# Two layers of a streaming encoder: a product, two squares and the last transposes issued in another order, and the output stored in eight half rows

## The reference

```python
for i in range(DEPTH):                    # DEPTH = 2
    if i % 2 == 0:
        x = x + s5_mixer(rmsnorm(x, s5_norm[j]), ...)       # state-space layer
    else:
        x = x + retention_mixer(rmsnorm(x, ret_norm[j]), ...)
    x = x + swiglu(rmsnorm(x, ffn_norm[i]), w_gate[i], w_up[i], w_down[i])
return rmsnorm(x, final_norm)

def swiglu(u, w_gate, w_up, w_down):      # hidden width 2816 = 22 tiles of 128
    h = silu(u @ w_gate) * (u @ w_up)
    return h @ w_down
```

## Times and profile before

| | us |
|---|---|
| median of 3 runs | 1261.93 |
| lowest, highest | 1260.85, 1262.49 |
| the profiled execution, device time | 1260.84 |
| its span | 1259.1 |
| PE busy, share of the span | 1219.4, 97% |
| VectorE busy | 856.3, 68% |
| ScalarE busy | 532.7, 42% |
| GpSimd busy | 64.1, 5% |

### The profile page before, as it was taken

How to read it: one execution, slowest core, us unless ns; L and a number is a source line. 1 busy time by engine, 2 the same in 40 slices (tenths; PEclk the granted TensorE clock), 3 DMA queues, 4 the chain that set the end, 5 groups by cost and what they waited for, 6 DMA issues and landing times.

```text
span 1259.1 us, 18813 instructions
## 1 busy us (share of the span) xinstructions
PE 1219.4 (97%) x7693; PEld 1071.1 (85%) x7693; DVE 856.3 (68%) x1009; ACT 532.7 (42%) x693; POOL 64.1 (5%) x84
## 2 busy tenths in 40 slices
PE   3889999999999999999999999999999999999997
PEld 3778879889988998888888888888879899989986
DVE  8997778578857867746555565643577578857865
ACT  5655555335523544333343333422454235523532
POOL 5950000000000000000000000000000000000000
PEclk9999999999999999999999999999999999999998
DMA  5663332323332323313323133233323333333321
GB/s 117 156 124 102 100 101 76 125 67 109 118 110 76 117 93 112 122 43 110 100 67 108 33 109 99 67 100 94 106 67 101 101 101 101 102 105 96 93 75 68
DMA packets 166521, 121.89 MB, mean 97 GB/s; under 512 B 6104, under 2 KB 158736, under 8 KB 166416
## 3 DMA queue, kind: packets, MB, share of 16 engines
q1 hardware_dynamic: 164784, 118.24, 31.1%
q10 hardware_dynamic: 1664, 2.62, 1.0%
HBM read 114.29 MB, written 2.10 MB: 92 GB/s over the span
## 4 chain that ended last, share of the span: by engine, by line
PE 93%; POOL 3%; DVE 2%; ACTq 1%; ACT 1%; issue 1%; DMA 0%; SPq 0%; DVEq 0%; POOLq 0%
PE bank L820 18%; PE bank L821 17%; PE bank L822 17%; PE bank L877 9%; PE bank L876 9%; PE bank L875 9%; PE bank L1002 2%; PE bank L1004 2%; PE bank L1003 2%; ACTq L518 1%; PE bank L1031 1%; PE bank L1030 1%; PE bank L1032 1%; PE bank L1041 1%; POOL s_pool_tmp L2147 1%
## 5 line engine op out<-in xcount | busy, mean ns | idle before, releaser
L1095 ACT ACTIVATE w_hi<-w_raw 128x2048 fp32r<-128x2048 f32 (+1 forms) x70 | 130.5, 1864 | 197.1 <-PE bank L822 178.2
L820 PE MATMUL bank<-u_hi,w_hi 128*128 128x512 f32 x480 | 188.4, 392 | 3.0 <-DVE tmp L1501 2.9
L822 PE MATMUL bank<-u_hi,w_lo 128*128 128x512 f32 x480 | 186.8, 389 | 0.0
L821 PE MATMUL bank<-u_lo,w_hi 128*128 128x512 f32 x480 | 186.8, 389 | 0.0
L1511 DVE TENSOR_TENSOR w_lo<-w_raw,w_hi 128x2048 fp32r<-128x2048 f32 x46 | 105.4, 2291 | 64.1 <-ACT w_hi L1095 64.0
L1501 DVE TENSOR_TENSOR tmp<-bank,tmp 128x512 f32<-128x512 f32 (+2 forms) x118 | 77.6, 659 | 95.1 <-PE bank L822 59.9
L875 PE MATMUL bank<-s_hi,w_hi 128*128 128x256 f32 x408 | 115.5, 283 | 0.0
L876 PE MATMUL bank<-s_lo,w_hi 128*128 128x256 f32 x408 | 115.5, 283 | 0.0
L877 PE MATMUL bank<-s_hi,w_lo 128*128 128x256 f32 x408 | 115.5, 283 | 0.0
L820 PE MATMUL bank<-hid_hi,w_hi 128*128 128x512 f32 x288 | 112.9, 392 | 0.9 <-issue 0.9
L822 PE MATMUL bank<-hid_hi,w_lo 128*128 128x512 f32 x288 | 112.2, 389 | 0.0
(11 more groups left out here) (274 smaller groups left out, 2743.7 us busy)
## 6 DMA issues: line engine op xcount, KB each, us to landing
w_raw<-in_ret_w_qkvg_dram SPq DMA_DIRECT2D x24, 1024.0 KB, 5.0
w_raw<-in_ffn_w_up_dram SPq DMA_DIRECT2D x44, 512.0 KB, 3.8
w_raw<-in_ffn_w_gate_dram SPq DMA_DIRECT2D x44, 512.0 KB, 4.8
w_raw<-in_ffn_w_down_dram SPq DMA_DIRECT2D x16, 1024.0 KB, 5.1
w_raw<-in_ret_w_o_dram SPq DMA_DIRECT2D x8, 1024.0 KB, 5.3
w_raw<-in_ffn_w_down_dram SPq DMA_DIRECT2D x8, 768.0 KB, 4.2
w_raw<-in_s_glu_w_dram SPq DMA_DIRECT2D x4, 1024.0 KB, 5.1
s<-in_x_dram ACTq DMA_DIRECT2D x8, 256.0 KB, 7.8
```

What stands on the lines that cost most here:

```text
L820: pe.matmul(o, w_hi[w][:, w_cols], hi, start=first, stop=False)
L821: pe.matmul(o, w_hi[w][:, w_cols], lo, start=False, stop=False)
L822: return pe.matmul(o, w_lo[w][:, w_cols], hi, start=False, stop=end)
L1095: return act.activation(o, i, ACT.Copy, scale=scale)
```

## The change

Four edits:

- VectorE, first plain units of both layers: `hidden(0)` moves from behind `gate_out(1)` to ahead of it, right behind `u_sums(layer, 0)`.
- VectorE, last unit of both layers: `down_out` and `next_norm` are done tile by tile (m = 0, then m = 1) instead of `down_out` for both tiles and then `next_norm` for both.
- PE, end of the program: the 16 transposes of the left halves are issued ahead of the column sums of `sq_sum` (and of the wait for `sum_done`) instead of behind them.
- The store: SP stores only the right halves, four DMAs of 256 KB, each when VectorE has written it; ScalarE issues the four DMAs of the left halves, each behind its own write of that half.

```diff
@@ SP
             for t in range(TT):
-                sp.wait_ge(out_left, t + 1)
                 sp.wait_ge(out_right, t + 1)
-                sp.dma_start(out[0, t * P:t * P + P, :], out_sb[:, t, :]).then_inc(out_stored, 16)
-            sp.wait_ge(out_stored, 16 * TT)
+                sp.dma_start(out[0, t * P:t * P + P, 512:D], out_sb[:, t, 512:D]).then_inc(out_stored, 16)
+            sp.wait_ge(out_stored, 16 * 2 * TT)
@@ PE
+            for t in range(TT):
+                transposed_steps(t, 0)
             pe.wait_ge(sum_done, (KT + 1) * 3 + KT)
             open_bank(7, FREE0["norm3"][7])
             last_columns(sq_sum, True, False)
-            for t in range(TT):
-                transposed_steps(t, 0)
             pe.wait_ge(sq_ready, KT * 4)
@@ ScalarE
                 act.activation(out_sb[:, t, 0:512], bank[2 * t][:, :], ACT.Copy,
                                scale=rs_col[:, t:t + 1]).then_inc(out_left, 1)
+                act.wait_ge(out_left, t + 1)
+                act.dma_start(out[0, t * P:t * P + P, 0:512], out_sb[:, t, 0:512]).then_inc(out_stored, 16)
@@ VectorE
-                def down_out(n):
+                def down_out(n, ms=(0, 1)):
...
-                    for m in range(2):
+                    for m in ms:
...
-                    dve.wait_ge(x_added, added + 2)
+                    dve.wait_ge(x_added, added + ms[-1] + 1)
-                def next_norm(n):
-                    for m in range(2):
+                def next_norm(n, ms=(0, 1)):
+                    for m in ms:
...
                             gate_out(n - 1)
                             u_sums(layer, 0)
+                            hidden(n - 1)
                             continue
                         gate_out(n - 1)
-                        if n == 2:
-                            hidden(n - 2)
-                        elif n == 3:
+                        if n == 3:
                             hidden_low(n - 2)
...
-                down_out(len(UNITS) - 1)
-                next_norm(len(UNITS) - 1)
+                for m in range(2):
+                    down_out(len(UNITS) - 1, (m,))
+                    next_norm(len(UNITS) - 1, (m,))
```

## The result

| us | before | after |
|---|---|---|
| median of the comparison | 1261.39 (4 runs, 1259.99 to 1262.49) | 1252.91 (4 runs, 1252.08 to 1253.19) |
| ratio | | 0.9932, interval 0.9915 to 0.9949 |
| profiled execution, its span | 1260.84, 1259.1 | 1252.99, 1251.2 |
| last FFN matmul's end to ScalarE's root (X) | 8.16 | 3.46 |
| X to the end of the span | 8.68 | 8.23 |

The kernel is 8.5 us faster, 6.4 to 10.7 by the interval, and the forecast was 1253.2. In all that follows X is the start of the root on ScalarE, as in the prediction.

What follows compares the result with a forecast made beforehand. PE was taken to bound the kernel, with gains at its waits ahead of unit 2 and the chain behind its last matmul. 3.3 + 4.8 + 0.6 = 8.7 us off the 1261.93 median gave 1253.2, range 1251.4 to 1256.8.

Steps and rivals of the forecast that it cites:

- Part 1: First units of both layers: earlier hidden(0) removes PE's wait ahead of unit 2, 3.3 us.
- The cover: Unit 2's start: time by which bank 1 is free before PE needs it, 0.3 to 0.5 us.
- rival 1: First units: PE's two stalls stay in whole or part, costing up to 3.3 us, 1256.5; chance 0.10.
- the restart of PE: Unit 2's first matmul takes 0.47 instead of 0.39 us; without it, the gain is 3.4 at best.
- Part 2: VectorE's tile-by-tile end: worth nothing in layer 0; in layer 1 the last square ends at 1244.42 instead of 1245.55.
- Parts 2 and 3: Program's end: tile-by-tile finish and transposes first bring X 4.8 us earlier, bounds 2.2 to 5.2.
- The assumption of the full clock up to X: Program's end: with transposes filling PE's gap, 16 transposes take 1.75 us and eight column-sum passes 0.79.
- rival 2: Program's end: TensorE drops to half clock right behind the FFN, gain 2.2 instead of 4.8, 1255.8; chance 0.09.
- Part 4: The store in half rows: first issue 0.67 us earlier, 0.1 lost in the flow, net 0.6.
- part 3: Program's end: PE's 16 left transposes run right behind the last FFN matmul, in 1.75 us instead of 2.96.
- rivals 3 to 5: Store: ScalarE's issues become the tail, 1255.8, 0.10; small stores don't overlap, 1257.1, 0.04; slow ScalarE queue, 1264.1, 0.02.
- rival 4: Store: small stores don't overlap in one queue, 3.9 us behind the forecast, 1257.1; chance 0.04.

Runs made afterwards that it cites:

- a1: Kernel before with only hidden(0) moved ahead of gate_out(1); 1258.06 us, ratio 0.9978.
- e1: Kernel before with eleven unread products put into PE's idle time behind the last FFN matmul; 1258.93 us beside 1261.03, ratio 0.9983.
- b1: Kernel before with only VectorE's tile-by-tile end of the last unit; 1257.49 us, ratio 0.9973.
- b4: Kernel before with the tile-by-tile end, and the norm's column sums in bank 5 instead of bank 7; one run, 1256.81 us beside 1261.03.
- f1: Changed kernel with the old store, four transfers of whole rows issued by SyncE; 1252.29 us, ratio 0.9935.
- b2: Kernel before with only PE's 16 transposes moved ahead of the first column sums; 1257.37 us, ratio 0.9971.
- c1: Kernel before with only the store in eight half rows, the left ones issued by ScalarE; 1260.82 us, ratio 0.9997.
- before_again: Kernel before, unchanged and profiled once more; one run, root 7.61 us behind the last FFN matmul.
- c2: Changed kernel with all eight half-row transfers issued by SyncE, none by ScalarE; one run, 8.20 us from X to the end.

## Why the prediction was right, and where not

- **What bounds the kernel.** Right: PE's waits, and the chain behind its last matmul. Both places moved as written, and nothing else in P did.
- **Part 1, 3.3 us.** Right in mechanism; 3.6 measured (P of a1 and of the changed kernel). The cover of 0.3 to 0.5 us held in both layers in each of the seven profiles that have this part (P is 1084.87 to 1085.00 in all), so rival 1 fell. The sum left out the restart of PE, which it had named as the upper end, 3.4. The measured 3.6 lies 0.2 above even that, and no run shows where these 0.2 come from; P of kernels with the old order differs by as much from profile to profile (1088.32 to 1088.53).
- **Part 2, nothing in layer 0.** Right (a1: P is already that of the changed kernel).
- **Parts 2 and 3, 4.8 us up to X.** 4.7 in the profile: X came 3.46 behind the FFN, 3.36 forecast; the 16 column-sum passes took 1.69 where 2 x 0.79 was reckoned. The assumption of the full clock up to X held, so rival 2 fell. The term was priced against the profile of before alone, though, and that profile is at the long end: the old order takes 6.31 us with the clock full, and 7.61 to 8.16 in the three with a fall. Rightly divided, 2.85 us are the order (6.31 less 3.46), and the rest is the clock.
- **Part 4, 0.6 us: wrong, it is 0.** This step failed. The prediction took the first store at X + 1.86 as a property of the old store. It came from VectorE's wait of 0.56 for transposes at half clock, which part 3 had already taken away. Of the 0.67 gained at the start 0.16 are left, and the 2 KB rows lose 0.2 and not 0.1. The profile's 0.45 between X and the end is the clock's share too (e1, b1, b4 and f1 have the old store and 8.17, 8.13, 8.18, 8.21). ScalarE's issue was priced too high, 0.34 to 0.38 and not 0.66, its copy too low (0.69 against 0.61), and neither decided anything: rivals 3 to 5 fell. The estimate of 2.6 us for a DMA of 256 KB beside rival 4 comes from a fit that the Trainium skill (DMA: Bandwidth & Descriptors, Anatomy of one DMA) gives for DMAs issued by GpSimd; here SyncE and ScalarE issue, the eight DMAs overlap, and they land at a median of 2.9 and 3.2 us behind their issue.
- **The sum.** By the experiments: 3.6 for `hidden(0)`, 2.85 for the order of the tail at full clock, 2.1 for the clock (e1, 0.9 to 3.3), 0 for the store: 8.55, against 8.48 in the medians. The clock's term is known to 1.2 us only, so the agreement to 0.1 is luck. The prediction had 8.7. The clock's 2.1, or most of it, comes with either of b1 and b2, since each cuts PE's idle time to 0.9 and the clock holds up to the root: at full clock b1 saves 1.8 (12.65 from the FFN to the end, against 14.48 in e1), and 1.8 + 2.1 is near its 3.5; b2 likewise saves 1.5, with a fall behind the root in it. That is why two edits worth 3.5 each are worth 5 together.
- **The total.** It came out right partly because two errors of size cancel: the store's 0.6 too much, `hidden(0)`'s 0.3 too little, and the clock's share was 2.3 us in the one execution that it was read from (1.85 ahead of X, 0.5 behind), near the 2.1 of the medians; read from a profile whose clock stayed full, as c1's did, the sum would have been about 2 us lower.

What stays open: why the clock falls in one execution of an unchanged order and not in the next. e1 and the changed kernel show that with the idle time filled it held up to the root in every profile, not what decides whether the fall comes; and b2 shows a fall right behind the root with 0.89 us of idle time, so no length of idle time is shown to be safe.

## What to carry to other kernels

Before pricing the edits of a tail one by one, ask which of its durations depend on the clock, and price each edit again with the durations that the others leave: two of three terms here rested on the same fall. Where an engine waits for an instruction that is queued behind a wait for that same engine, look whether the instruction's inputs are there earlier; that was 3.6 of the 8.5 us. An idle stretch of PE ahead of a dependent chain can cost time beyond its own length, and filling it, with useful work if there is any, is a cheap test.

## What the runs showed of the hardware

- The granted clock at the end of an unchanged order differs between executions: full to the root in c1 (2.63 us of idle time), down to 0.5 in before_again 1.2 us ahead of the second column sums, and earlier in before. The Trainium skill (TensorE: Matmul & The Clock Gate, Part 1) has the clock halved after idle time, and the moment of a change differing from run to run. The four profiles agree with the second; to the first they add that the same idle time is followed by a fall or by none. So it is at a place in the first mixer, 56 to 60 us into the span: a fall in 10 of 14 profiles behind 1.9 to 2.5 us of idle time, and none in c2 and f1 behind 2.1 and 2.2.
- Behind its last FFN product PE does nothing but transposes and single-column passes in the changed kernel, and the granted clock stays full for all of it:

```profile
1239.50:1241.50 2.00, 2.00 (x22) 2.00 (x19) 1.87 (x3) 0.51 (x1) 0.00 (x0) 1.00 0.00 0
1241.50:1243.00 1.50, 1.50 (x15) 1.50 (x16) 0.00 (x0) 0.15 (x2) 0.00 (x0) 1.00 0.00 0
1243.00:1244.80 1.80, 1.74 (x16) 1.50 (x14) 1.44 (x3) 1.10 (x3) 0.00 (x0) 1.00 0.01 5
```

  The prediction had left open whether it would. Whether such work alone could raise a clock that has fallen was not tried.
- Overlapped stores of 128 rows moved at 404 to 407 GB/s with rows of 2 KB and at 423 with rows of 4 KB, with the DMA engines busy throughout. Four pieces of 128 KB from one engine were paced by their issue, 0.5 us each: 262 GB/s at a DMA share of 0.75.
